# Linear attention's levels: the remainders of two weight units computed by GpSimd, and half units of the value and gate products dealt out anew between the levels

## The reference

```python
proj = h @ w_in                      # q, k (4 heads x 128), v, g (4 heads x 256), low-rank gates
la_f = log_sigmoid(lr_f @ w2[0] + b[0]) / 16        # and la_b: a log decay per token, head, feature
# o_i = sum_{j<=i} (q_i * exp(b_i - b_j)) . k_j v_j,   b = cumsum(log_a)   (forward)
# and the same backward over j > i
o = rms_norm(o_f + o_b, o_norm_g) * silu(g)
return o @ w_out
```

## Time and profile before

| what | value |
|---|---|
| median of 3 runs | 1364.3 us (1364.17 to 1365.05) |
| the profiled execution's own time | 1364.36 us |
| its span, first to last instruction | 1362.5 us |
| mean granted TensorE clock | 0.999 of full speed |
| TensorE busy | 1340.8 us, 98% |
| VectorE busy | 970.2 us, 71% |
| ScalarE busy | 724.7 us, 53% |
| GpSimd busy | 120.9 us, 9% |

### The profile page before, as it was taken

How to read it: one execution, slowest core, us unless ns; L and a number is a source line. 1 busy time by engine, 2 the same in 40 slices (tenths; PEclk the granted TensorE clock), 3 DMA queues, 4 the chain that set the end, 5 groups by cost and what they waited for, 6 DMA issues and landing times.

```text
span 1362.5 us, 18898 instructions
## 1 busy us (share of the span) xinstructions
PE 1340.8 (98%) x7725; PEld 1162.8 (85%) x7725; DVE 970.2 (71%) x1133; ACT 724.7 (53%) x979; POOL 120.9 (9%) x175
## 2 busy tenths in 40 slices
PE   7999999999999999999999999999999999999998
PEld 7888889888888888888888889888888878888887
DVE  6788876966687777677776877566576776765554
ACT  6444458555544455444456766544455566644443
POOL 2100000300000000000015112000014001100000
PEclk9999999999999999999999999999999999999999
DMA  8877645424877657878655426555534203265551
GB/s 291 285 258 257 220 139 186 155 93 151 306 254 247 216 185 233 284 264 265 205 170 191 155 94 233 186 187 185 187 119 143 63 32 124 96 226 195 193 186 62
DMA packets 166900, 256.20 MB, mean 188 GB/s; under 512 B 4915, under 2 KB 135262, under 8 KB 163614
## 3 DMA queue, kind: packets, MB, share of 16 engines
q1 hardware_dynamic: 164414, 248.63, 54.7%
q0 software_dynamic: 2240, 6.31, 1.8%
q10 hardware_dynamic: 160, 0.05, 0.0%
HBM read 253.65 MB, written 1.32 MB: 187 GB/s over the span
## 4 chain that ended last, share of the span: by engine, by line
PE 72%; DVE 6%; ACT 4%; POOL 2%; issue 2%; DVEq 0%; POOLq 0%; ACTq 0%
PE acc L224 22%; PE banks L617 20%; PE banks L627 11%; PE banks L577 2%; PE banks L186 2%; PE banks L188 2%; PE banks L187 2%; DVE w_lo L177 2%; ACT w_hi L171 2%; PE banks L607 1%; POOL rstd L1501 1%; DVE arena L886 1%; PE banks L1035 1%; POOL mean_sq L1498 1%; PE acc L2533 1%
## 5 line engine op out<-in xcount | busy, mean ns | idle before, releaser
L177 DVE TENSOR_TENSOR w_lo<-w_raw,w_hi 128x2048 fp32r<-128x2048 f32 x212 | 486.8, 2298 | 117.4 <-ACT w_hi L171 116.6
L171 ACT ACTIVATE w_hi<-w_raw 128x2048 fp32r<-128x2048 f32 x212 | 405.0, 1910 | 57.4 <-PE banks L188 15.3
L617 PE MATMUL banks<-h_both,w_hi 128*128 128x512 f32 x1520 | 370.7, 391 | 0.0
L617 PEld LDWEIGHTS banks<-h_both,w_hi 128*128 128x128 f32 x1520 | 278.8, 188 | 53.6 <-issue 0.9
L627 PEld LDWEIGHTS banks<-h_both,w_lo 128*128 128x128 f32 x1520 | 194.9, 191 | 7.4
L627 PE MATMUL banks<-h_both,w_lo 128*128 128x256 f32 x1520 | 197.2, 283 | 0.0
L224 PE MATMUL acc<-w_lo,act_hi 128*128 128x512 f32 x400 | 155.9, 390 | 0.0
L224 PE MATMUL acc<-w_hi,act_hi 128*128 128x512 f32 x400 | 155.8, 390 | 0.0
L224 PE MATMUL acc<-w_hi,act_lo 128*128 128x512 f32 x400 | 155.8, 390 | 0.0
L471 ACT ACTIVATE silu_gate<-banks 128x512 f32<-128x512 f32 x55 | 32.9, 599 | 156.0 <-PE banks L617 139.0
L485 ACT ACTIVATE act_hi<-act 128x512 fp32r<-128x512 f32 x50 | 31.5, 630 | 138.9 <-PE acc L224 138.9
(11 more groups left out here) (351 smaller groups left out, 1999.3 us busy)
## 6 DMA issues: line engine op xcount, KB each, us to landing
w_raw<-in_ffn_w_gu SPq DMA_DIRECT2D x88, 1024.0 KB, 5.2
w_raw<-in_ffn_w_down SPq DMA_DIRECT2D x44, 1024.0 KB, 5.0
arena<-in_w_ada SPq DMA_DIRECT2D x24, 1024.0 KB, 6.4
w_raw<-in_w_ffn_in SPq DMA_DIRECT2D x22, 1024.0 KB, 5.1
w_raw<-in_gla_w_in SPq DMA_DIRECT2D x12, 1024.0 KB, 5.2
w_raw<-in_diff_w_in SPq DMA_DIRECT2D x12, 1024.0 KB, 5.2
w_raw<-in_w_ffn_out SPq DMA_DIRECT2D x11, 1024.0 KB, 4.9
w_raw<-in_w_in SPq DMA_DIRECT2D x9, 1024.0 KB, 5.1
```

The source lines that it names most:

```text
L171: eng.activation(w_hi[:, slot, :], w_raw[:, slot, :], ACT.Copy).then_inc(sem("unit_hi"), 1)
L177: eng.tensor_tensor(w_lo[:, slot, :], w_raw[:, slot, :], w_hi[:, slot, :].bitcast(F32), ALU.subtract).then_inc(sem("unit_split"), 1)
L617: return pe.matmul(outs[ct], hi[:, k, ct * P:(ct + 1) * P], h_both[:, k, :, t], start=k == 0, stop=k == KT - 1)
```

## The change

GpSimd makes the remainders of units 10 and 12 after its totals. VectorE keeps 11, now after level 2 (where it had 11 before too), and makes 13 behind the last level, directly ahead of 14. The helper `split_lo` is the same; before each remainder where the engine changes, a wait on `unit_split` keeps the order of the counter. The table `behind` deals the same ten half units out anew: two at level 0 and at level 2, one at each other level (before: two at levels 2 and 5).

```diff
@@ gla_vector, the levels @@
                 kept(level)
-                if level in (1, 2):
-                    split_lo(eng, u + 9 + level)
-                elif level in (4, 5):
-                    split_lo(eng, u + 8 + level)
+                if level == 2:
+                    eng.wait_ge(sem("unit_split"), u + 11)
+                    split_lo(eng, u + 11)
+            eng.wait_ge(sem("unit_split"), u + 13)
+            split_lo(eng, u + 13)
             split_lo(eng, u + 14)
@@ gla_pool, behind the totals @@
+            u = base[name]
+            pool.wait_ge(sem("unit_split"), u + 10)
+            split_lo(pool, u + 10)
+            pool.wait_ge(sem("unit_split"), u + 12)
+            split_lo(pool, u + 12)
@@ gla_tensor @@
-            behind = (((7, 1),), ((8, 0),), ((8, 1), (9, 0)), ((9, 1),), ((10, 0),), ((10, 1), (11, 0)), ((11, 1),),
+            behind = (((7, 1), (8, 0)), ((8, 1),), ((9, 0), (9, 1)), ((10, 0),), ((10, 1),), ((11, 0),), ((11, 1),),
                       ((12, 0),))
```

## The result

The changed kernel took 1374.5 us in the median of 4 runs (1371.9 to 1375.0), the kernel before 1364.4 us in 4 runs on the same chip (1364.2 to 1365.1). The medians differ by 10.1 us; the ratio, which goes by all the runs, is 1.0069 with a 95% interval of 1.0057 to 1.0081. So the change is slower. The forecast was slower by 4.1 us, with a range that ended at 1372.5. So the sign came as forecast and the size did not.

What follows compares the result with a forecast made beforehand. TensorE, busy 98% of the span, was taken as the bound. The order (-2.9) and the holds at levels 1 (+2.8) and 4 (+4.2) summed to +4.1 us, a median of 1368.4 us, range 1363.5 to 1372.5.

Steps and rivals of the forecast that it cites:

- TensorE is the bound, and any new standstill is lost at full price: Whole kernel: TensorE is busy 98% of the span, so only its standing time can be won.
- The order, -2.9 us if VectorE is unhindered: Levels: the new half-unit order, with three remainders moved from between VectorE's levels, removes all standing of TensorE, -2.9 us.
- GpSimd's remainder, 4.2 us taken, 3.8 to 13.8 kept: Length of one 128x2048 remainder on GpSimd: 4.2 us, four times its 128x512; low end 3.8, high end 13.8 us.
- It holds off the weightings for whole instructions: Levels: GpSimd's remainder keeps VectorE's weightings, with two SBUF operands, waiting for up to 4.2 us.
- The rival of no exclusion: Levels: long GpSimd instructions do not hold off VectorE's weightings, so the change brings -2.9 us, 1361.4 us; chance 0.12.
- that of VectorE keeping the port: Level 4: VectorE, starting first, keeps the port through its four weightings; sum +2.1 us, 1366.4 us; chance 0.12.
- Levels 1 and 4, 2.8 and 4.2 us: Levels 1 and 4: GpSimd's remainder delays the weightings, so TensorE loses 2.8 us and 4.2 us.
- TensorE has stood from 258.3: 2.65 us, and restarts 0.16 us slower: Level 1: TensorE waits 2.65 us for keys, join and latency, then its scores take 1.90 for 1.74 us; 2.8 us.
- Behind 300 us everything is shifted by the same: After the levels: all work comes later by the same amount as L1165, forecast at 295.3 instead of 291.15.
- A difference that arises after 300 us: Behind the levels: a listed sign that the forecast is wrong; no size given.
- The sum: Whole kernel: -2.9 for the order, +2.8 and +4.2 for levels 1 and 4, +4.1 us in all.

Runs made afterwards that it cites:

- hardly any remainder: The changed kernel with GpSimd's two remainder subtractions over 16 of 2048 columns, waits and counts unchanged; 1363.28 us (10 runs), ratio 0.9992 to the kernel before.
- the remainders alone: The kernel before with GpSimd making remainders 10 and 12 as in the change, but the old table of half units; 1376.3 us (4 runs), ratio 1.0088.
- the four pieces: The changed kernel with each of GpSimd's two remainders as 4 instructions of 512 columns; 1373.1 us (4 runs), ratio 1.0063 to the kernel before.
- the filled waits: The changed kernel with 11 and 18 needless matmuls where TensorE would stand, ahead of the scores of levels 2 and 5; 1370.25 us (4 runs), ratio 1.0044.
- the third kernel above: The changed kernel with GpSimd's remainders in three pieces between weightings, plus a needless 128x256 matmul ahead of each small mixer matmul; 1366.65 us (11 runs).

## Why the prediction was right and wrong

- *TensorE is the bound, and any new standstill is lost at full price*: right, and more than full price.
- *The order, -2.9 us if VectorE is unhindered*: right in kind, 0.7 us too much. With hardly any remainder no wait is left in the levels and they are 2.2 us shorter, since a level with one half unit takes 4.56 to 4.71 us where I had 2.79 + 1.74 = 4.53.
- *GpSimd's remainder, 4.2 us taken, 3.8 to 13.8 kept*: 4.58. The Trainium skill's 4497 ns ("GPSIMD Engine Reference", section 3.1) was nearer than my four times 1.04 us; this case's rows agree with it within 2%. A row that I had already read was as near: the 2.0 us of the 128x896 behind 34.75, taken times 2048/896, is 4.6 us, and not 4.2.
- *It holds off the weightings for whole instructions*: right up to 4.58 us, in the earlier trace rows shown for 1.04 us only. The rule of the Trainium skill, "SBUF — State Buffer", section "SBUF: two separate sides" (an exclusive lock for the whole instruction) agrees. The rival of no exclusion is out by the changed kernel, that of VectorE keeping the port by the remainders alone, where VectorE was first and had to give way after one weighting.
- *Levels 1 and 4, 2.8 and 4.2 us*: the standstills came as 2.63 and 4.05 us, 6.7 in two pieces as forecast, put down to the weighting and not to the join. From the scores of level 1 to those of level 2 it was 7.44 us, where the forecast's times (260.95 - 253.8) make 7.15; at level 4 8.85 against 8.55. So the two terms were 0.6 us short in all, 0.3 each: the remainder was 0.38 us longer and began 0.13 and 0.14 us later behind the scores, and the chain behind the hold took 2.43 us (258.68 to 261.11) where I had 2.65. That chain was described incompletely: it also has the queries' weightings in it. In the changed kernel these end with the join, within 0.02 us; in the four pieces they ended 1.1 us after it and set the time.
- *"TensorE has stood from 258.3: 2.65 us, and restarts 0.16 us slower"*: **this is the step that failed.** The price of a standstill was put at its length and 0.16 us, from a restart behind 1.2 us. What it left out is the granted clock behind a standstill two and three times as long: 4.0 us by the rows, 3.9 us by the filled waits. The levels of before could not show it, with a clock of 1.00 and no standstill over 1.2 us. But the end of the same trace did. TensorE's last matmul ends at 1356.8 us, and then the clock falls while it does nothing, in the first stretch of one microsecond that is under 1.00 (busy, clock, DMA share, GB/s):

```profile
1360.00:1361.00 1.00, 0.00 (x0) 0.59 0.73 272
```

That was reason to give a standstill beyond 1.2 us an open upper end.
- *Behind 300 us everything is shifted by the same*: wrong by 1.55 us, for the mixer's spell. The forecast had no term for it. "A difference that arises after 300 us" was listed as a sign of error, and it was one, though the runs of before have the spell too, in part.
- *The sum*: 4.1 forecast, + 0.6 for the two holds, + 4.0 for the clock and + 0.2 in the other levels is 8.9 us, by which the levels grew (51.87 us from 248.07 to 299.94, before 42.96). With 0.1 us less at the entry and 0.1 more up to the mixer, and the 1.55 us there, it is the 10.5 us between the spans. The sign of the result was no luck, for both holds came as forecast; and even without the spell in the mixer the time would have been some 4.5 us above the forecast.

## What to carry to other kernels

When TensorE is busy all the time, price a new standstill of some microseconds at its length and at the slow clock behind it; here the second was as much as 60% of the first. Before work with SBUF operands goes to GpSimd, look whether VectorE's two-operand work starts within its length: a piece placed behind VectorE's own last such instruction, while it copies from PSUM, cost nothing here, whereas cutting it up without placing it brought the time back to that of before with pieces of 128 columns, and hardly helped with 512. And of a semaphore chain ask for every producer that the next consumer waits for, not only for the longest one.

## What the runs showed of the hardware that was not expected

- The granted clock fell to 0.5 with standstills of 2.63 us (low for 3.4 us) and 4.05 us (low for 6.8 us, of which 1.2 before the restart) in a kernel whose TensorE is 98% busy. Behind 2.72 us in the four-piece kernel it did not fall, so the border is not sharp in the length of the standstill. The Trainium skill, "TensorE: Matmul & The Clock Gate", Part 1, ties the clock to how busy TensorE has been; the filled waits agree.
- When both engines have two-operand SBUF work queued, they take turns instruction by instruction, with pieces of 128 (0.9 us a turn of both) as of 512 columns (1.7 us), and a remainder of 2048 columns gets its turn after one weighting of VectorE that had started first.
- A one-input copy on GpSimd (128x2048 in 1.89 us, less than half of the subtraction's 4.58) holds VectorE's two-operand work as well, by 1.5 us in the one execution seen; VectorE's masked copies from PSUM are not held (1.35 to 1.38 beside a piece, 1.34 alone).
- The clock fell in the mixer in some executions of one and the same kernel and not in others, at 1 to 1.6 us each. In the changed kernel it fell a microsecond after a pause of 0.5 us; in the third kernel above it fell with no wait of TensorE anywhere near.
